# One issuing engine for all value units of a hybrid decoder step, and its stores moved behind the weight tiles

## The reference

```python
def token_mix(xn, ...):
    proj = xn @ w_in                                   # q, k, v, z, x/B/C, dt
    q, k = apply_partial_rope(q, pos), apply_partial_rope(k, pos)
    attn = rmsnorm(attend(q, k, v), g_attn)            # samples: 2 cached pages of 128 rows each
    xbc, conv_new = causal_conv(xbc, conv_state, ...)
    y, ssm_new = ssd_scan(xs, dt, a, b_in, c_in, ssm_state)
    y = _rms(... (y + d_skip * xs) * silu(z)) * g_ssd
    out = jnp.concatenate([attn, y], axis=-1) @ w_out
    return out, k, v, conv_new, ssm_new
# then x + out, a norm, and the PEER layer: scores against sub-keys, top 16 of 16384 experts per head,
# gelu(x . u_e) * gate * v_e over the chosen experts, then the final norm
```

## Time and the profile before

| what | value |
|---|---|
| median of three runs | 1171.94 us (1170.41 to 1173.0) |
| the profiled execution's own time | 1171.42 us |
| its span in the trace | 1169.7 us |
| PE busy | 1144.1 us (98%) |
| DVE, ACT, POOL busy | 768.0, 604.8, 738.3 us |
| DMA | 225.13 MB, mean 192 GB/s |

### The profile page before, as it was taken

How to read it: one execution, slowest core, us unless ns; L and a number is a source line. 1 busy time by engine, 2 the same in 40 slices (tenths; PEclk the granted TensorE clock), 3 DMA queues, 4 the chain that set the end, 5 groups by cost and what they waited for, 6 DMA issues and landing times.

```text
span 1169.7 us, 24328 instructions
## 1 busy us (share of the span) xinstructions
PE 1144.1 (98%) x7599; PEld 1011.1 (86%) x7599; DVE 768.0 (66%) x1686; ACT 604.8 (52%) x1388; POOL 738.3 (63%) x610
## 2 busy tenths in 40 slices
PE   8999999789899999999999999999999999999997
PEld 7888787569788999999999999998888888888876
DVE  6787676952399996003899999984454466665534
ACT  3355554843355555564555544445555555555545
POOL 0032221737365998998666667666677798788754
PEclk9999999998999999999999999999999999999999
DMA  7578766784453766656554444445666697688643
GB/s 240 177 236 277 225 216 197 244 316 145 144 161 93 219 186 187 185 159 199 144 143 140 143 144 139 143 145 154 189 189 189 188 327 265 231 275 294 190 153 108
DMA packets 108668, 225.13 MB, mean 192 GB/s; under 512 B 12754, under 2 KB 21570, under 8 KB 108074
## 3 DMA queue, kind: packets, MB, share of 16 engines
q1 hardware_dynamic: 104706, 210.50, 58.0%
q0 software_dynamic: 2944, 10.49, 2.5%
q10 hardware_dynamic: 936, 3.14, 0.7%
HBM read 215.80 MB, written 8.19 MB: 192 GB/s over the span
## 4 chain that ended last, share of the span: by engine, by line
PE 72%; issue 1%; DVE 0%; POOL 0%; ACT 0%; DVEq 0%; POOLq 0%; ACTq 0%
PE bank L1747 31%; PE bank L1777 30%; PE bank L1757 5%; PE bank L1700 2%; PE bank L1712 1%; PE bank L1724 1%; PE bank L1797 0%; PE bank L1814 0%; POOL hl L1640 0%; DVE acts L2173 0%; PE bank L1805 0%; ACT acts L1983 0%; POOL hl L1625 0%; PE bank L1832 0%; PE bank L1790 0%
## 5 line engine op out<-in xcount | busy, mean ns | idle before, releaser
L1625 POOL TENSOR_TENSOR hl<-ring,hl 128x512 fp32r<-128x512 f32 x448 | 587.1, 1321 | 184.3 <-ACT hl L1863 176.5
L1863 ACT CAST hl<-ring 128x512 fp32r<-128x512 f32 x512 | 317.1, 620 | 290.5 <-PE bank L1777 156.8
L1747 PE MATMUL bank<-split,hl 128*128 128x256 f32 x3072 | 378.4, 282 | 0.4 <-ACT hl L1863 0.3
L1747 PEld LDWEIGHTS bank<-split,hl 128*128 128x128 f32 x3072 | 366.2, 188 | 0.8 <-issue 0.5
L1777 PE MATMUL bank<-hl,split 128*128 128x512 f32 x1524 | 353.6, 394 | 0.0
L1777 PEld LDWEIGHTS bank<-hl,split 128*128 128x128 f32 x1524 | 286.0, 188 | 67.7 <-issue 0.9
L528 PE MATMUL pj<-xn,ring 128*128 128x264 f32 x672 | 156.7, 388 | 0.7 <-ACT proj L833 0.7
L2143 DVE TENSOR_TENSOR split<-acts,split 128x256 fp32r<-128x256 f32 x128 | 130.5, 1044 | 37.9 <-ACT split L1959 33.7
L528 PEld LDWEIGHTS pj<-xn,ring 128*128 128x128 f32 x672 | 125.0, 190 | 24.2 <-issue 4.4
L2150 DVE TENSOR_TENSOR hl<-ring,hl 128x512 fp32r<-128x512 f32 x64 | 46.6, 729 | 116.7 <-ACT hl L1863 116.7
L2109 DVE TENSOR_SCALAR bv<-bkey,ig 128x130 f32<-128x130 f32 x256 | 86.0, 394 | 0.0
(11 more groups left out here) (369 smaller groups left out, 1113.7 us busy)
## 6 DMA issues: line engine op xcount, KB each, us to landing
ring<-in_uv SPq DMA_DIRECT2D x256, 256.0 KB
ring<-in_v_rows SPq DMA_DIRECT2D x256, 256.0 KB
ring<-in_w_ring SPq DMA_DIRECT2D x76, 512.0 KB, 4.3
room<-in_cache_k SPq DMA_DIRECT2D x64, 128.0 KB, 2.7
hs<-in_state_ssm SPq DMA_DIRECT2D x8, 512.0 KB, 5.6
out_ssm_s<-hs SPq DMA_DIRECT2D x8, 512.0 KB, 6.3
acts<-x_rows SPq DMA_DIRECT2D x8, 512.0 KB, 5.4
room<-in_cache_v SPq DMA_DIRECT2D x12, 256.0 KB, 5.7
```

Of the source, the lines that this page charges most:

```text
L1625: nc.gpsimd.tensor_tensor(hl[:, r % HL, 1], raw[:, r], hl[:, r % HL, 0].bitcast(F32), ALU.subtract).then_inc(lo_done, 1)
L1747: mm = nc.tensor.matmul(out, hl[:, r % HL, m, k * P:(k + 1) * P], split[:, x, kk, 0:TP], start=(kk == 0 and n == 0), stop=(kk == KD - 1 an ...
L1863: nc.scalar.copy(hl[:, r % HL, 0], raw[:, r]).then_inc(hi_done, 1)
```

## The change

All value units are issued by SP, in order of use: 1, 0, then (between the first weight tiles) 5, 2, 3, 4, and 6 and 7 last. POOL issues none. Unit 5 gets a home of its own in the part of `proj` that held the SSD inputs; so the cast of the attention half now waits until unit 5 is used (`unit_used, KU + 6`). On PE the last two key units come ahead of `attend(6)`, and value units and output halves alternate more evenly. ACT does the sample exponentials first and casts weight pieces earlier; DVE does the last step of the prompt attention (`masked(7)`) after the SSD part's `mix_low`, and `sample_factors` and `values_kept(1)` ahead of the norm of the attention half; the two `mix_low` of the prompt's attention half now follow the sample attention. The stores of keys, values and prompt states come behind the tiles 48 to 63.

```diff
-        V_HOME = (2, 3, 4, 0, 1, 2, 4, 0)
+        val_homes.append(part(proj[:].rearrange("p k n -> p (k n)"), X0 * NT, SIDE, D // 2))
+        V_HOME = (2, 3, 4, 0, 1, 5, 4, 0)
...
+                    elif n == 5:
+                        sp.wait_ge(y_done, KD)
+                        sp.wait_ge(ys_done, KD)
                     else:
-                        sp.wait_ge(unit_used, {4: KU, 5: KU + 1, 6: KU + 3, 7: KU + 4}[n])
+                        sp.wait_ge(unit_used, {0: KU - 2, 3: KU - 1, 4: KU, 6: KU + 3, 7: KU + 4}[n])
...
                             values(1)
+                            values(0)
...
                 tile(N_IN)
+                tile(N_IN + 1)
+                values(5)
+                tile(N_IN + 2)
                 values(2)
-                tile(N_IN + 1)
+                values(3)
                 values(4)
-                for i in range(N_IN + 2, N_IN + RING):
-                    tile(i)
+                tile(N_IN + 3)
                 state_out(KD - 1)
...
-                for n in range(5, VU):
+                for n in (6, 7):
                     values(n)
+                for i in range(N_IN + RING, N_IN + N_OUT + RING):
+                    sp.wait_ge(o_lo, 2 * (i - N_IN - RING) + 2)
+                    sp.dma_start(ring[:, i % RING], t["w_ring"][i].rearrange("p (a b) -> p a b", a=KD)).then_inc(ring_full[i % RING], 16)
                 sp.wait_ge(qk_ready, 2 * KD)
                 store(sp, t["k_out"], proj[:, K0:K0 + KD])
...
                 store(sp, t["ssm_p"], h1[:])
-                for i in range(N_IN + RING, N_IN + N_OUT + RING):
...
                 for s in range(HS):
                     sp.wait_ge(hs_out[s], 16 * (KD // HS))
                 sp.wait_ge(out_done, 16 * outs[0])
@@ POOL
-                    if c == KD - 2:
-                        values(0)
...
-                values(3)
@@ PE
+                    if c == KD - 1:
+                        key_unit(KU - 2)
+                        key_unit(KU - 1)
                     if c:
                         attend(c - 1)
...
                         group_sums(0)
-                        key_unit(KU - 2)
-                        key_unit(KU - 1)
                         group_sums(1)
...
+                value_unit(5)
                 turn_probs(KD - 1)
-                value_unit(5)
-                attend(KD - 1)
+                value_unit(6)
                 pe.wait_ge(v6_masked, 2)
                 out_half(N_IN + 2, 2, 1, True, False)
+                attend(KD - 1)
+                value_unit(7)
+                out_half(N_IN + 3, 3, 1, True, False)
...
                 values(0)
-                value_unit(6)
-                out_half(N_IN + 3, 3, 1, True, False)
-                value_unit(7)
                 values(1)
@@ ACT
-                group_root(0)
                 for b in range(NQ):
                     sample_exps(b)
+                group_root(0)
+                act.wait_ge(sum_s, 2)
+                out_high(0, 2)
...
                 group_root(1)
-                out_high(0, 2)
                 ssd_high(0)
-                exps(KD - 1)
+                ssd_high(1)
+                out_high(2, 4)
...
-                ssd_high(1)
-                out_high(2, 4)
+                exps(KD - 1)
                 out_high(4, 6)
                 normal(KD - 1)
+                out_high(6, 8)
                 probs_out(KD - 1)
+                out_high(8, 10)
                 attended(KD - 1)
...
-                out_high(6, 8)
+                act.wait_ge(unit_used, KU + 6)
@@ DVE
-                ssd_scaled(0)
-                masked(KD - 1)
...
                 sample_rates()
+                ssd_scaled(0)
                 ssd_scaled(1)
...
-                recips(KD - 1)
...
+                masked(KD - 1)
                 values_kept(0)
+                recips(KD - 1)
+                sample_factors()
+                values_kept(1)
...
-                sample_factors()
...
-                values_kept(1)
-                for n in (0, 1):
-                    mix_low(n + 3, n, lows[n], slice(0, TP)).then_inc(mix_lo, 1)
...
                 nc.vector.tensor_tensor(mix[:, 0:KD, TP:NT], tmp6, o6[:], ALU.add).then_inc(att_s, 1)
+                for n in (0, 1):
+                    mix_low(n + 3, n, lows[n], slice(0, TP)).then_inc(mix_lo, 1)
```

More of the change, by code:

```diff
@@ L452, in _ @@
                 store(sp, t["ssm_p"], h1[:])
-                for i in range(N_IN + RING, N_IN + N_OUT + RING):
-                    sp.wait_ge(o_lo, 2 * (i - N_IN - RING) + 2)
-                    sp.dma_start(ring[:, i % RING], t["w_ring"][i].rearrange("p (a b) -> p a b", a=KD)).then_inc(ring_full[i % RING], 16)
                 for s in range(HS):
@@ L481, in _ @@
                     sums.then_inc(st_done, 1)
[L483 to L492, removed]
                 pool.wait_ge(st_done, KD)
-                pool.wait_ge(ptab_in, 16)
                 for c in range(KD - 1):
-                    if c == KD - 2:
-                        values(0)
                     pool.wait_ge(o_copied, 2 * c + 2)
@@ L997, in _ @@
                     else:
+                        spread(c)
                         squares(0)
@@ L1005, in _ @@
                     else:
-                        spread(c)
                         squares(1)
@@ L1061, in _ @@
                     nc.scalar.copy(mixr[:, 4 * n:4 * n + 4, 0:TP], mix[:, 4 * n:4 * n + 4, 0:TP]).then_inc(mix_hi, 1)
-                out_high(8, 10)
                 act.wait_ge(att_s, 1)
                 nc.scalar.activation(sq_att[:, :, TP:NT], mix[:, 0:KD, TP:NT], ACT.Square).then_inc(sq_l, 1)
-                out_high(10, 11)
+                out_high(10, 12)
                 act.wait_ge(var_l, 1)
                 nc.scalar.activation(rr[:, 0, TP:NT], rr[:, 0, TP:NT], ACT.Sqrt).then_inc(root_l, 1)
-                out_high(11, 12)
                 act.wait_ge(mixed_l, 1)
@@ L1343, in _ @@
                 nc.vector.tensor_tensor(qk6[:], proj[:, Q0:Q0 + KD, TP:NT], proj[:, K0:K0 + KD, TP:NT], ALU.mult).then_inc(qk6_ready, 1)
-                group_var(0)
                 dve.wait_ge(unit_used, KU)
@@ L1347, in _ @@
                 nc.vector.tensor_scalar(s6[:, 1], s6[:, 0], -SCALE, None, ALU.mult).then_inc(max6, 1)
+                group_var(0)
                 group_var(1)
```

## The result

The changed kernel takes 1178.37 us (1177.83 to 1179.82, 4 runs) against 1171.18 (1169.35 to 1173.0) for the kernel before: a ratio of 1.0063, 95% interval 1.0044 to 1.0083. It is slower by some 7.2 us, where the prediction said 1169.4 with a range to 1172.8. Every ratio in this document leaves out one execution of the kernel before in the slow state, 2294.72 us in the session of the first four experiments. The profiled execution took 1178.82 us with a span of 1176.9.

A forecast was written before the change was run, and what follows sets the result against it. PE was taken to bound the kernel over its whole span. Terms -9.0 + 6.0 + 0.7 = -2.3 us took the profiled 1171.42 to 1169.1; with the runs' median 0.5 above, it predicted 1169.4, range 1166.0 to 1172.8.

The forecast's parts named there:

- Part 1: Up to the first output half: PE's 4.8 us wait for value unit 0 goes; start 231.4 instead of 236.36, -5.0.
- Rival (c): SP's single list of value units: unit 3 lands at 232.5, PE pauses, gain 3.9 not 9.0; 1174.5 us, chance 0.11.
- Part 2: First output half to first attention half: DVE sets the pace; 265.3 against 274.30, -9.0 with Part 1 inside.
- Rival (d): Ahead of the attention half: a wait on reordered ACT leaves savings equal to the stores' cost; about 1171.7 us, chance 0.07.
- Part 3: End of the stage: stores behind the last tile land at 310.1, stage end was 304.14; +6.0, bounds 5.5 to 9.2.
- Part 4: Start of the next stage: PE's longer pause can lengthen the lower-clock stretch; +0.7 us, within 0 to 1.3.
- The front: Stretch up to the first attention half, forecast to start at 265.3 against 274.30: -9.0 us.

The follow-up runs named there:

- the first four experiments: Stores behind tile 63 in the kernel before (ratio 1.0062); changed kernel with stores ahead of tile 48 (1.0044), page numbers kept (0.9998), unit 3 on GpSimd (1.0029).
- both mends: Changed kernel with page numbers loaded once and kept, and the three stores behind tiles 53, 56 and 59: 1162.48 us, ratio 0.9927.

## Why the prediction was wrong

**Part 1, the first output half, and what SP issues behind it: the issue times of SP's list are the step that failed.** The prediction read "Four value DMAs cost SP 3.63 us" off a row that runs from the first DMA to the last and put units 2, 3 and 4 end to end at that price, which gave 225.2 and 228.8. The true price is 4.4 us a unit, since four DMAs need four page loads and the row holds three. The old trace had shown it: there the tile ahead of a unit is out at 221.19 and the unit's first DMA starts 0.77 us later (SP's timeline of the kernel before):

```profile
220.76 0.43 SPq L341 DMA_DIRECT2D ring<-in_w_ring  x1
221.96 3.61 SPq L385 DMA_DIRECT2D room<-in_cache_v  x4
```

The error adds up along one queue. Unit 4 was out at 234.09, which is 233.5 on the clock of the kernel before (less the 0.63 by which the fixed points differ), 4.7 us later than forecast, and PE waited 5.65 us for units 3, 4 and 6. That removing the page loads removes exactly these waits is shown by the run with the pages kept. The prediction had compared rates (290 against 384 GB/s asked and granted). It did hold SP's finish time against PE's demand, but for unit 3 alone and at the low price (landing 228.5, wanted 228.2), never for units 4 and 6. Rival (c) had the mechanism, one queue for all units, but a wrong reason (a landing of 7.6 us; for units 3 and 4 it was 3.1 to 4.5) and only unit 3 in it. Its 1174.5 left out units 4 and 6. Two signs that the prediction named as "wrong" came: unit 3 waiting for a DMA, and the lower clock ahead of 262 (mean 0.67 from 259 to 262). No run tried unit 5 issued behind unit 4. PE uses it last of these four, and its place in SP's list holds 4.4 us of issue ahead of units 2, 3 and 4, so that order is an untested other way to bring units 3 and 4 in time.

The first half itself was forecast rightly, partly by luck. The forecast of 231.4 is 160.9 from the fixed point; with the pages kept the half began at 161.1, behind DVE, and in the changed kernel at 162.3, behind unit 3. Two errors in DVE's time made each other good. The eight products of the norm took 5.35 us where 3.3 were counted, and an operation on 128x2 elements that had taken 2.37 us in the old list took 0.16. DVE's timelines of the changed kernel and of the kernel before, and POOL's of the changed kernel:

```profile
225.50 5.35 DVE L1368 SCALAR_TENSOR_TENSOR mix<-mix,par,att 128x264 f32<-128x264 f32 x8
```
```profile
228.77 2.37 DVE L1354 TENSOR_TENSOR s<-s 128x2 f32<-128x2 f32 x1
```
```profile
225.44 2.69 POOL L502 TENSOR_TENSOR wo<-ring,wo 128x512 fp32r<-128x512 f32 x2 [4.86 <-ACT wo L1016]
```

Two of the eight products took 1.5 us each, and they are the two that ran beside POOL's two subtractions; the other six took 0.48. That the two engines held each other up is my reading of the overlap; no run separated it.

**Part 2, from there to the first attention half.** Once the units came in time the number was near and the last step was not the one that was forecast. On the clock of the kernel before (less 1.45) the run with the pages kept has its sums ready at 250.5 (forecast 250.7), the products done at 256.6 (256.8) and the first attention half at 264.35 (265.3). Two `mix_low` took 3.5 us instead of 2.4, of which the 0.7 added for blocking covers most. From the late sum to the last `mix_low` it was 1.65 us instead of 3.8: the two small ones took 0.19 and 0.18 where the old trace had 1.17 and 1.31. So DVE was done 1.2 us before the half began, and what ended last was PE's own sixth SSD half. That the total came within a microsecond is in part luck. In the changed kernel the same stretch also met a later tile 48 (cast at 253.37 after 8.5 us of waiting). It cost PE nothing there because PE was itself late: the sums could have started at 255.6 and started at 256.83. Rival (d) had named this wait on ACT; the runs with the stores ahead of tile 48 show it.

**Part 3, the stores.** The mechanism was right, and named as the cost of the change; the size was 6.0 and measured 7.4, inside the bounds of 5.5 and 9.2. Tile 63 went out at 299.4 and SP was released at 311.3: 11.9 us, where 10.1 were counted. The bytes went faster than the 384 GB/s assumed; it is the two ends that take longer. Windows of the changed kernel:

```profile
300.50:301.00 0.50, 0.50 (x7) 0.50 (x5) 0.00 (x0) 0.00 (x0) 0.00 (x0) 1.00 0.32 66
...
304.00:304.50 0.50, 0.00 (x0) 0.00 (x0) 0.00 (x0) 0.00 (x0) 0.00 (x0) 1.00 1.02 430
...
309.00:309.50 0.50, 0.00 (x0) 0.00 (x0) 0.00 (x0) 0.00 (x0) 0.00 (x0) 0.50 0.61 247
309.50:310.00 0.50, 0.00 (x0) 0.00 (x0) 0.00 (x0) 0.00 (x0) 0.00 (x0) 0.50 0.05 16
```

Full rate is reached only after 302, and SP is released 1.8 us after the last busy window, where the kernel's last store had left 1.4 us for everything. At the measured 420 GB/s the 3.21 MB take 7.6 of the 11.9 us. The fixed part is therefore about 4.3, and the term that was sized wrong is the 1.7 taken for it. The Trainium skill, page "DMA: Bandwidth & Descriptors", section "Anatomy of one DMA — SWDGE (gpsimd) path", puts a fixed cost of about 2.0 us on a DMA of GpSimd's path. These stores were SP's, so the figure was carried over to another path, and the 4.3 us measured here are twice that.

**Part 4, the clock.** +0.7 was forecast within 0 to 1.3, and the first two tiles took 9.47 instead of 9.04: +0.4. Behind pauses of 10.69 and 10.71 us in two other runs they took 10.29 and 10.37, at the upper bound, so the 0.4 is what this one execution gave.

**The sum.** Forecast -9.0 + 6.0 + 0.7 = -2.3; measured from the fixed point -1.1 + 7.4 + 0.4 = +6.7, and 0.6 of start. (From the median of 1171.94 the forecast sum gives 1169.6, not 1169.4; it changes nothing here.) The front is 7.9 us off, the stores 1.4. The error of the stores alone would have stayed within the range; the one of the front alone would have left it. The rivals were each priced with the other terms at their forecast, so no case held a poor front and dear stores together, which is what came.

## What to carry to other kernels

When one queue takes over the issue of several engines, write its finish time for every transfer in order of use, with everything between two issues counted (the first register load as well), and compare each with the time its user is ready; a comparison of rates does not show a queue that falls behind. A store that a stage's end waits for cost nothing that showed at the one spacing tried among the last loads, and its fixed part and its bytes behind them. Two edits that look independent can share a queue: here the same change made the front depend on the place of the stores, so each should be tried in both settings of the other. And a pause costs more than its length: PE's work behind it can run at the lower clock.

## What the runs showed of the hardware

- A page number loaded into a register and the DMA that uses it take SP 0.91 us; with the number kept, eight such DMAs of 256 KB took 4.33 us, 0.54 each. At the first pace the changed kernel moved 288 GB/s from 223.7 to 233.45; at the second the DMA engines were full (401 GB/s from 224 to 228), and every unit was there when PE wanted it.
- A pause of the same 2.90 us between the stages left the lower clock in one kernel and not in another: the two tiles behind it took 9.04 us with both mends and 7.36 in the changed kernel with early stores. The price of such a pause was uncertain by 1.7 us here.
- Three stores of 2.69 MB ran at a mean of 420 GB/s from 302.5 to 309.0, but from 300 to 302, right behind their issue, the DMA engines moved 66 to 188 GB/s, and SP was released 1.8 us after the last busy window.
- A DVE operation on 128x32 elements took 1.17 and 1.31 us in the kernel before, while POOL was at work on weight pieces (its row runs from 271.67 to 276.69), and 0.19 and 0.18 in the changed kernel, where POOL stood from 271.32 to 272.90.
